# An expert layer with another order of passes, its end, and the next layer's pieces held back

## What is computed

```python
def moe_ffn(h, w_router, e_bias, w_gate, w_up, w_down, s_gate, s_up, s_down):
    scores = jax.nn.sigmoid((h @ w_router).astype(jnp.float32))
    _, idx = lax.top_k(scores + e_bias.astype(jnp.float32), TOP_K)
    wts = jnp.take_along_axis(scores, idx, axis=-1)
    wts = wts / wts.sum(-1, keepdims=True) * ROUTE_SCALE
    ...
    def expert_block(args):
        tok, e = args
        xb = h_pad[tok]
        a = jax.nn.silu(xb @ w_gate[e]) * (xb @ w_up[e])
        return a @ w_down[e]
    ...
    routed = jnp.zeros((n_tok + 1, d), h.dtype).at[slot_tok].add(y)[:n_tok]
    shared = (jax.nn.silu(h @ s_gate) * (h @ s_up)) @ s_down
    return routed + shared

# in both layers of the second network
x = layer_norm(DN_ALPHA * x + g1 * y, ln1_g[l], ln1_b[l])
h2 = x * (1.0 + sc2) + sh2
x = layer_norm(DN_ALPHA * x + g2 * ff, ln2_g[l], ln2_b[l])
```

## Time and profile before

| | us |
|---|---|
| median of 3 runs (3505.86 to 3507.59) | 3506.56 |
| the profiled execution | 3510.23 |
| its span | 3508.5 |
| PE busy | 3232.0 (92%) |
| DVE busy | 1368.3 (39%) |
| POOL busy | 396.4 (11%) |
| PE's granted clock, mean | 0.97 |
| chain that ended last: PE 73%, DMA 13%, DVE 7%, issue 4% | |
| HBM read | 846.28 MB |

### The profile page before, as it was taken

The page is one execution under the profiler, slowest core; times in us unless marked ns, Lnnn a source line. Parts: engine busy times, 40 slices in busy tenths (PEclk is TensorE's granted clock), DMA queues, the critical chain, the costliest instruction groups (busy, mean ns, idle before and its releaser), DMA issues.

```text
span 3508.5 us, 39750 instructions
## 1 busy us (share of the span) xinstructions
PE 3232.0 (92%) x14346; PEld 2180.2 (62%) x14346; DVE 1368.3 (39%) x3065; ACT 522.9 (15%) x1094; POOL 396.4 (11%) x452
## 2 busy tenths in 40 slices
PE   7999989999999998999999988999985999989897
PEld 5888868888888887888564433343433576333333
DVE  4766434565025565576463322222213033111112
ACT  2200122001011003100132111111111021101111
POOL 0000021001010000000121211121112101000000
PEclk8999999999999999999999999999997999999999
DMA  7687524774436772576100589999994214999996
GB/s 297 242 328 289 211 96 173 296 286 156 150 118 239 290 269 76 192 258 253 62 13 36 203 301 383 375 371 348 354 364 166 112 37 182 395 411 411 414 407 249
DMA packets 135155, 860.79 MB, mean 245 GB/s; under 512 B 20416, under 2 KB 23872, under 8 KB 37440
## 3 DMA queue, kind: packets, MB, share of 16 engines
q1 hardware_dynamic: 94128, 665.89, 48.3%
q0 software_dynamic: 40128, 191.41, 15.8%
q10 hardware_dynamic: 720, 1.13, 0.1%
HBM read 846.28 MB, written 35.13 MB: 251 GB/s over the span
## 4 chain that ended last, share of the span: by engine, by line
PE 73%; DMA 13%; DVE 7%; issue 4%; ACT 1%; POOL 1%; SPq 0%; POOLq 0%; DVEq 0%; ACTq 0%
PE ps L764 14%; PE ps L1114 13%; DMA ring<-stream_in 10%; PE ps L1393 10%; PE ps L1095 9%; PE ps L861 8%; PE ps L1417 6%; PE ps L1435 2%; PE ps L1354 1%; DVE arena L1932 1%; DMA arena<-mod_stream_in 1%; PE ps L776 1%; PE ps L819 1%; PE ps L828 1%; PE ps L1216 1%
## 5 line engine op out<-in xcount | busy, mean ns | idle before, releaser
L1393 PE MATMUL ps<-ring,arena 128*64 128x512 f32 (+2 forms) x2112 | 578.2, 647 | 112.5 <-DMA ring<-stream_in 103.2
L1393 PEld LDWEIGHTS ps<-ring,arena 128*64 128x64 f32 (+2 forms) x2112 | 206.1, 154 | 431.6 <-issue 425.6
L1932 DVE SCALAR_TENSOR_TENSOR arena<-arena,cond 128x512 f32<-128x512 f32 x602 | 426.7, 749 | 88.6 <-DMA arena<-mod_stream_in 79.4
L1114 PE MATMUL ps<-arena,ring 128*128 128x256 f32 x2048 | 445.1, 379 | 4.5 <-DVE arena L2246 4.5
L1114 PEld LDWEIGHTS ps<-arena,ring 128*128 128x128 f32 x2048 | 387.9, 190 | 57.5 <-issue 5.5
L1095 PE MATMUL ps<-H,ring 128*128 128x256 f32 x1920 | 421.7, 380 | 0.2
L1095 PEld LDWEIGHTS ps<-H,ring 128*128 128x128 f32 x1920 | 363.4, 191 | 50.1 <-issue 1.7
L1417 PE MATMUL ps<-ring,arena 128*64 128x512 f32 (+2 forms) x1056 | 287.9, 609 | 20.4 <-issue 13.6
L1583 ACT ACTIVATE arena<-ps 128x512 f32<-128x512 f32 (+2 forms) x339 | 172.2, 508 | 767.1 <-PE ps L764 318.4
L2453 DVE TENSOR_TENSOR arena<-arena,ps 128x256 f32<-128x256 f32 x76 | 32.0, 422 | 642.1 <-ACT arena L1813 642.1
L1417 PEld LDWEIGHTS ps<-ring,arena 128*64 128x64 f32 (+2 forms) x1056 | 95.5, 146 | 185.1 <-issue 173.0
(11 more groups left out here) (284 smaller groups left out, 3263.3 us busy)
## 6 DMA issues: line engine op xcount, KB each, us to landing
ring<-stream_in SPq DMA_DIRECT2D x612, 1024.0 KB
arena<-mod_stream_in POOLq DMA_DIRECT2D x130, 1024.0 KB, 5.1
arena<-mod_stream_in SPq DMA_DIRECT2D x8, 1024.0 KB, 13.2
YS<-mod_stream_in SPq DMA_DIRECT2D x6, 1024.0 KB, 5.3
arena<-stream_in SPq DMA_DIRECT2D x4, 1024.0 KB, 5.9
moe_out<-zeros POOLq DMA_DIRECT2D x10, 256.0 KB, 4.2
stat<-stream_in SPq DMA_DIRECT2D x2, 1024.0 KB, 5.1
moe_in<-YS POOLq DMA_DIRECT2D x1, 2048.0 KB, 7.6
```

The lines of the kernel that those rows point to most:

```text
L1114: m = mm(out[:, i * T:(i + 1) * T], w[:, c * P:(c + 1) * P], f_h[:, 16 * half + c, :], start=(half == c == 0), stop=(half == 1 and c == 15))
L1393: m = mm(out[at, :], e_xt[:, k % 2, 4 * part + c, at], w[:, c * TC:(c + 1) * TC], start=(part == c == 0), stop=(part == 1 and c == 3))
L1932: ins = stt(acc, w, x, acc, MUL, ADD)
```

## The change

1. The first layer's passes come in another order, with the same kinds (28 S, 20 P): `SSPPPP`, four times `HOSP`, `S`, seven times `SSP`, `SPSS`. H is the first pass of a heavy rank (0 to 3), O its second, in lane A, shared with a light rank (28 to 31) in lane B; before, the two heavy ranks of a `three_for_two` shared theirs. A pass's ranks have each their own first row (`firsts`).
2. DVE's `count_spares`, with the reading of the count, moves from ahead of the first pass to the start of pass 2, in both layers; POOL reads the count at pass 3; POOL's `scale_residual` is split, one of eight operations in each of the passes 3 to 10.
3. The last pass's scatter goes to lane B, has a semaphore of its own and waits for no other scatter. Lane A's four loads wait for the scatters before it, lane B's four loads (instead of one of 2 MB) for it.
4. SP sends the next layer's pieces only when all eight of those loads have landed.
5. The layer norms' two sums use PSUM banks 0 and 1 instead of 6 and 7.

```diff
-        order["ln", 2 * l] = Phase([6, 7], 0)
+        order["ln", 2 * l] = Phase([0, 1], 0)
...
-        order["ln", 2 * l + 1] = Phase([6, 7], 0)
+        order["ln", 2 * l + 1] = Phase([0, 1], 0)
...
-def three_for_two(r):
-    return [Round((r,)), Round((r + 1,)), Round((r, r + 1), P)]
...
-    first = three_for_two(0) + pair(28) + pair(30) + three_for_two(2) + pair(32) + pair(34)
...
+    def in_turn(kinds, at, light=0):
         rounds = []
         for kind in kinds:
-            made, count = {"S": (solo, 1), "P": (pair, 2), "Q": (quad, 4)}[kind]
-            rounds += made(at[kind])
-            at[kind] += count
+            if kind == "O":
+                r = at["H"] - 1
+                rounds.append(Round((r, light + r), (P, 0)))
+            else:
+                count = {"H": 1, "S": 1, "P": 2, "Q": 4}[kind]
+                rounds.append(Round(tuple(range(at[kind], at[kind] + count))))
+                at[kind] += count
         return rounds
 
-    first += in_turn("SP" * 3 + "SSP" * 10 + "PS", {"S": 4, "P": 36})
+    first = in_turn("SSPPPP" + "HOSP" * 4 + "S" + "SSP" * 7 + "SPSS", {"H": 0, "S": 4, "P": 32}, 28)
...
+        lane_ready = [(ff_set, 16 * 12), (h2_stored, 16 * 4)] + [(full, 16 * (mod_loads_of_half + 1)) for full in mod_full]
...
             for l in range(DEPTH_2):
+                if l:
+                    for tb in range(TC // P):
+                        sp.wait_ge(ff_loaded[tb], 32)
+                        sp.wait_ge(*lane_ready[tb])
                 for p in range(at, PLAN["moe", l].first):
                     fixed(p)
...
                     if l == 0 and rounds[k].pair:
                         ts(slot_out[:, at], token, V("slot", 3), None, ADD)
+                    elif l == 0 and k == len(rounds) - 1:
+                        ts(slot_out[:, at], token, float(FAR + LANE_B), None, ADD)
...
-                count_spares(l, nb)
-                n_spare = spares(dve, l)
...
-                for b in range(2):
-                    with dve.If(n_spare > b):
-                        spare_pick(b, b)
                 rows_turned(0)
...
                 for k in range(len(rounds)):
+                    if k == 2:
+                        count_spares(l, nb)
+                        n_spare = spares(dve, l)
+                        for b in range(2):
+                            with dve.If(n_spare > b):
+                                spare_pick(b, b)
...
                 for tb in range(nb):
-                    dve.wait_ge(lane_loaded, 16)
                     dve.wait_ge(ff_loaded[tb], 32)
+                    dve.wait_ge(*lane_ready[tb])
                     tt(e_acc[:, tb, :], e_acc[:, tb, :], lane_rows[:, tb, :], ADD).then_inc(sums_ready, 1)
...
                 gather(0)
                 gather(1)
-                scale_residual(2 * l + 1)
                 gather(2)
                 gather(3)
...
                 for k in range(len(rounds)):
                     gather(k + 4)
+                    if 3 <= k < 3 + DC:
+                        scale_residual(2 * l + 1, k - 3)
+                    if l and k == 3:
+                        n_spare = spares(pool, l)
+                        first_picks()
...
-                        wait_past(pool, scattered, 16 * k)
-                        if k == last_pair + 1:
-                            pool.dma_start(lane_rows[:, 0:nb, :], ff[LANE_B:LANE_B + cols].rearrange("(a p) n -> p a n", p=P))\
-                                .then_inc(lane_loaded, 16)
+                        if k < n_rounds - 1:
+                            wait_past(pool, scattered, 16 * k)
...
-                        rows = slot_out if rounds[k].pair else slot_token
+                        rows = slot_out if rounds[k].pair or k == n_rounds - 1 else slot_token
...
+                            .then_inc(scattered if k < n_rounds - 1 else lane_loaded, 16)
                 if l == 0:
-                    pool.wait_ge(scattered, 16 * len(rounds))
+                    pool.wait_ge(scattered, 16 * (n_rounds - 1))
...
                 for tb in range(nb):
                     pool.dma_start(e_acc[:, tb, :], ff[tb * P:(tb + 1) * P]).then_inc(ff_loaded[tb], 16)
+                pool.wait_ge(lane_loaded, 16)
+                for tb in range(nb):
+                    pool.dma_start(lane_rows[:, tb, :], ff[LANE_B + tb * P:LANE_B + (tb + 1) * P]).then_inc(lane_ready[tb][0], 16)
```

More of the change, by code:

```diff
@@ L243, with __init__ @@
 class Round:
-    def __init__(self, ranks, first=0):
-        self.ranks, self.first = ranks, first
+    def __init__(self, ranks, firsts=None):
+        self.ranks, self.firsts = ranks, firsts or (0,) * len(ranks)
         self.pair = len(ranks) == 2
@@ L467, in build @@
         ff_loaded = [sem(f"ff_loaded{tb}") for tb in range(4)]
+        mod_loads_of_half = 1 + sum(len(m["jobs"]) * m["turns"] for key, m in MOD_PLAN.items() if key[0] in ("up", "down"))
+        lane_ready = [(ff_set, 16 * 12), (h2_stored, 16 * 4)] + [(full, 16 * (mod_loads_of_half + 1)) for full in mod_full]
         spares_counted = sem("spares_counted")
@@ L2415, in one_hot @@
                         wait_filled(dve, ph, SLOT, k - 2)
-                    for r, at in rounds[k].lanes:
+                    for (r, at), first in zip(rounds[k].lanes, rounds[k].firsts):
                         for tb in range(nb):
                             out, places, n = onehot[:, k % 2, tb, at], count1[:, 0:at.stop - at.start], rank[:, tb, r:r + 1]
-                            if rounds[k].first:
-                                last = ts(out, places, n, -float(rounds[k].first), SUB, ALU.is_equal)
+                            if first:
+                                last = ts(out, places, n, -float(first), SUB, ALU.is_equal)
                             else:
@@ L2740, in scale_residual @@
                     pool.wait_ge(hm_pool, 8 * n + 8)
-                for c in range(DC):
-                    pool.wait_ge(hm_dve, 8 * n + c + 1)
-                    g.tensor_scalar(X[:, c, 0:cols], X[:, c, 0:cols], DN_ALPHA, None, MUL).then_inc(x_alpha, 1)
+                pool.wait_ge(hm_dve, 8 * n + c + 1)
+                g.tensor_scalar(X[:, c, 0:cols], X[:, c, 0:cols], DN_ALPHA, None, MUL).then_inc(x_alpha, 1)
             def layer_norm(m, cols):
@@ L2782, in moe @@
                 pool.dma_start(h2[0:cols].rearrange("(a p) n -> p a n", p=P), h2_rows[:, 0:nb, :]).then_inc(h2_stored, 16)
-                pool.wait_ge(h2_stored, 48 * (l + 1))
+                pool.wait_ge(h2_stored, 48 + 64 * l)
                 rounds, before = MOE[l].rounds, rounds_before(l)
-                last_pair = max(k for k, rd in enumerate(rounds) if rd.pair)
+                n_rounds = len(rounds)
+                assert l or not (rounds[-1].pair or rounds[-2].pair)
                 def gather(k):
@@ L2906, in _ @@
                     modulate_context(2 * l)
-                scale_residual(2 * l)
+                for c in range(DC):
+                    scale_residual(2 * l, c)
                 if l == 0:
```

17 lines of the change are left out of this document (7 added, 10 removed).

## The result

The changed kernel takes 3453.84 us (median of 4 runs, 3447.56 to 3458.47) against 3506.21 for the one before beside it (3503.05 to 3507.59): ratio 0.9851, 95% interval 0.9834 to 0.9868, some 52 us less. The forecast was 3467 (40 less), its own range 3455 to 3478, the range for all cases 3443 to 3487.

The account below looks back on a forecast made before the run. The weight stream bounds the first expert layer, except its first 150 us, where full ring slots block sending. Order with count -24, end -12, banks -4.8 and +0.8 make -40: 3467 us, range 3455 to 3478, 8 in 10 3443 to 3487.

Parts of the forecast that it names:

- What bounds the layer: First expert layer: bound by the weight stream, except the first 150 us, where full ring slots idle DMA; 52.5 us idle.
- Part 1, the order: First expert layer: new pass order empties ring slots earlier; 24 us less, including 5.6 from the earlier start.
- the walk: Hand simulation of both pass orders in the first expert layer: 27 us idle for the change, PE's end at 2629.5.
- Part 2, the count: First layer's start: without the spare-block count the first product begins 5.6 us earlier; at pass 2 it costs 0.
- Part 3, the end: First expert layer's end: last scatter waits for no other, lane loads and DVE's adds come earlier; 12 us less.
- Part 4, the held pieces: Start of the next layer: pieces held until all eight loads land arrive in time for the first product; cost 0.
- Part 5, the banks: Layer norms: sum over X no longer waits for late-drained banks, 4.8 us saved; last norm loses 0.8.
- a): First expert layer: the order gives only the earlier start, steady groups not paced by bytes; -22, 3485 us; chance 0.12.
- b): First expert layer's end gives nothing, as lane B is read after the last scatter; -28, 3479 us; chance 0.10.
- e): First expert layer: heavy experts holding three slots each shut the ring, making it slower; +11, 3518 us; chance 0.05.
- d): Next layer's start: it waits for its held pieces, all 20 us exposed; 3487 us; chance 0.05.
- c): First expert layer: all early DMA idle goes, -48 there; total 3443 us; chance 0.08.

Follow-up runs that it names:

- d_first: Changed kernel with one old three (two heavy ranks sharing a pass) at the very start, new groups after it: 3471.0 us, 0.9905 of the kernel before.
- c_start: Changed kernel with its start SSPPPP kept, its four HO groups replaced by two old threes: 3468.3 us, 0.9893 of the kernel before.
- b_order: Kernel before with only the new order of passes (and `firsts`, which it needs): 3479.3 us, ratio 0.9927.
- a_old: Changed kernel with the old order of passes, heavy ranks in threes, only the last group SPPSS: 3482.9 us, 0.9934 of the kernel before.
- a_count: Changed kernel with the count of spare blocks ahead of DVE's first copy again, in both layers: 3451.6 us, 0.9843 of the kernel before.
- a_nohold: Changed kernel without the hold, SP sending the next layer's pieces as slots come free: 3457.6 us, 0.9863 of the kernel before.

## Why the prediction was right, and where it was off

- **What bounds the layer**: right. With the same 192 pieces the layer and its start got 40.6 us shorter, of which 35.5 are idle time of the DMA engines that is gone, and d_first and c_start lost it again with holes in the DMA share.
- **Part 1, the order: the term that was mis-sized.** 18.4 us were predicted beside the start's 5.6; the changed kernel shows 34.8, b_order 33.8, a_old 31.3 by undoing it. Two steps of the walk fell. It left 27 us of idle where 18 are left: before 1980 it was right (11.3 us, walked 12), behind that it had 15 where the windows show 6.7 and next to nothing from 2000 on. And it let PE trail the last piece by 5 us more, since the last two passes are single experts. PE's tail behind the last piece's issue is 24.9 against 24.5: not longer. The "11 us" came from the walk alone, no row stood behind it. The two make 14 of the 16 missing us; the rest fits the steady groups, 40.1 us each instead of 40.8, and a first product at the full clock (2.7 us), but is not settled.
- **The walk's match with the kernel before was in part luck.** It met the idle time and PE's end (53 and 2653.5), but not the piece between them: it has 6 us of PE's work behind the last piece, so that piece at some 2647, and the prediction's sum has it at 2648. SP issued it by 2629.72. In the changed kernel the DMA share falls from 1.00 to 0.70 within the 5 us from 2595, so the piece issued by 2591.34 had landed by some 2599; with the same delay it landed before at some 2637 (estimates from these rows). So the walk had the stream's end 10 us late and PE's tail as much too short; for the change it had them at 2619 and 11, where the rows give some 2599 and 17. And by the rule of its own bound (idle that is gone, less 5 for the tail) 27 us of idle are worth 21, not 24.
- **Part 2, the count**: the size was right (5.8 for 5.6), the reason only half of it. I priced the count at the length it had in the trace, without asking what ran beside it on POOL. At pass 2 it takes 4.9 us (2010.68 to 2015.57) and costs nothing that the runs can tell, as predicted: a_count, which does not have it there, has a layer of 658.7 us. POOL's 76 gathers take 988 to 1128 ns at the engine, as before.
- **Part 3, the end**: -10.4 for -12. The scatter was shorter than I took it (6.24 for 7.5, done at E + 7.1), the loads longer: first add at E + 14.1 and not at E + 12. The first add waits for one block of each lane, the fifth of the eight loads. That load was issued at 2623.64 and took 6.7 us to land, where I had some 4, from the loads of the kernel before, which had no others ahead of them. Here lane A's four (2.1 MB, 5 us at the 422 GB/s of the earlier trace rows) had been issued from 2620.26 on and took 5.0 to 7.1 us each, so most of their bytes still stood ahead; that this is the reason is argued, no run moves lane B's loads alone.
- **Part 4, the held pieces**: cost 0, as said; the first product that reads one, at 2662.00, had no wait, 27.8 us after SP sent the first. What the prediction had not set apart is what the hold gives: 7 of the 10 us of part 3.
- **Part 5, the banks**: 4.6 of wait for 4.8, and 2.0 more that I left out, since PE without the wait keeps its full clock (7.10 us for 9.14). The 0.8 lost in the last norm came as computed.
- **Rivals**: a), b) and e) fall, by the layer's length, by the 10.4 us of the end, and by the share of 1.02 between 2070 and 2110. Without the hold b) would nearly have come true (2.7 us). d) falls. c) (all early idle goes) came nearer than I gave it: two thirds of it went. Of the wrong signs that I had named, a falling share between passes 6 and 20 did show, as a single dip of 4 us, and a steady group takes 40.1 us, not 40.8; both are small.

## What to carry to other kernels

When a ring of buffers feeds a stream-bound stage, look at what each early step keeps shut: a pass that holds most slots for a later one costs a hole, here of 5 to 16 us, and in c_start and d_first the layer was longer by about as much. The price of a chain of small operations can depend on what the neighbour engine does at that time (8.6 us here beside POOL's scalings, 4.7 without); before pricing its removal, look beside it. In a tail where nothing else is to be done, count the bytes that stand ahead of the awaited ones: here prefetches that were not needed for another 25 us were better held back, by 7 us at the first add.

## What I had not expected of the hardware

- DVE and POOL side by side were slower than DVE alone: eight subtractions of 128 x 512 took 6.8 us shared out, 4.91 on DVE by itself. A copy of 128 x 2 went from 0.17 to 0.79 us beside POOL's scalings.
- The granted clock fell to 0.50 for some 3 to 4 us under the same sixteen products in five of fourteen traces, and stayed at 1.00 in the other nine, with the same 2.17 us of idle ahead of them. The fall costs 1.4 to 1.5 us and can hide a gain of that size in a single trace.
- An accumulating scatter of 128 rows takes 6.24 us with the engines nearly free, 11.46 beside a stream of 1 MB pieces (a_nohold), and behind a load of 2 MB and beside pieces 11.59 in the kernel before but 19.8 in b_order.
